# Attention stages of a two-layer streaming encoder: chunks turned and multiplied two at a time, with one PSUM bank for outputs instead of two

## The reference, cut to what matters

```python
def fox_attention_prompt(q, k, v, logf):
    ...
        s = jnp.einsum('bqhd,bkhd->bhqk', qb, k).astype(jnp.float32) * scale
        s = s + cq[..., :, None] - cum[..., None, :]
        ...
        p = jax.nn.softmax(s, axis=-1).astype(v.dtype)
        return jnp.einsum('bhqk,bkhd->bqhd', p, v)

def band_attention_prompt(q, k, v, rel_bias):
    ...
        s = jnp.einsum('bqhd,bkhd->bhqk', qs, ks).astype(jnp.float32) * scale + bias
        ...
        p = jax.nn.softmax(s, axis=-1).astype(vs.dtype)
        return jnp.einsum('bhqk,bkhd->bqhd', p, vs)
```

## Time and profile before

| what | value |
|---|---|
| median of three runs | 3223.16 us (3222.48 to 3224.68) |
| the profiled execution, its own time | 3227.8 us |
| its span, first to last instruction | 3226.0 us |
| PE busy over the span | 3075.5 us, 95% |
| DVE busy over the span | 1371.6 us, 43% |
| ACT, POOL busy | 1062.1 us (33%), 396.3 us (12%) |
| attention phase fox, on PE | 405.9 to 687.5 us |
| attention phase band, on PE | 1997.6 to 2258.6 us |

### The profile page before, as it was taken

One profiled execution on the slowest core, in us unless ns is written; L12 is line 12 of the kernel. 1 busy time (PEld: TensorE's weight loads), 2 busy tenths in 40 slices (PEclk: granted clock), 3 DMA queues, 4 the chain that ended last, 5 costly groups with the idle time before them and its releaser, 6 DMA issues. The chain is left out here.

```text
span 3226.0 us, 49287 instructions
## 1 busy us (share of the span) xinstructions
PE 3075.5 (95%) x16891; PEld 2779.7 (86%) x16891; DVE 1371.6 (43%) x2948; ACT 1062.1 (33%) x2313; POOL 396.3 (12%) x702
## 2 busy tenths in 40 slices
PE   8999699989999999999999998999889999999998
PEld 7877489977899999999978886888779999999998
DVE  3122179962433343333342221888343333333334
ACT  4233178851412121111133232787231111211212
POOL 0000056620000000000000001666010000000001
PEclk9999899999999999999999998999989999999999
DMA  4788165523311111111026875563111111111111
GB/s 152 202 229 237 49 229 211 186 103 100 151 40 44 60 39 52 39 39 39 1 72 187 253 202 174 180 236 134 53 66 53 39 39 39 39 39 39 39 46 59
DMA packets 317139, 337.61 MB, mean 105 GB/s; under 512 B 29009, under 2 KB 260449, under 8 KB 312817
## 3 DMA queue, kind: packets, MB, share of 16 engines
q1 hardware_dynamic: 317040, 336.31, 32.5%
HBM read 238.46 MB, written 111.54 MB: 108 GB/s over the span
## 5 line engine op out<-in xcount | busy, mean ns | idle before, releaser
L230 PE MATMUL ffn_gu<-ffn_xh,ffn_gh 128*128 128x384 f32 x2112 | 708.5, 335 | 0.0
L232 PE MATMUL ffn_gu<-ffn_xh,ffn_gl 128*128 128x384 f32 x2112 | 707.5, 335 | 0.0
L231 PE MATMUL ffn_gu<-ffn_xl,ffn_gh 128*128 128x384 f32 x2112 | 707.1, 335 | 0.0
L1496 ACT ACTIVATE ffn_gate<-ffn_gu 128x384 f32<-128x384 f32 x132 | 65.0, 492 | 1035.4 <-PE ffn_gu L232 1035.3
L230 PEld LDWEIGHTS ffn_gu<-ffn_xh,ffn_gh 128*128 128x128 f32 x2112 | 397.6, 188 | 2.4
L231 PEld LDWEIGHTS ffn_gu<-ffn_xl,ffn_gh 128*128 128x128 f32 x2112 | 397.4, 188 | 2.4
L232 PEld LDWEIGHTS ffn_gu<-ffn_xh,ffn_gl 128*128 128x128 f32 x2112 | 397.2, 188 | 0.0
L1500 DVE TENSOR_TENSOR ffn_gate<-ffn_gu,ffn_gate 128x384 f32<-128x384 f32 x132 | 73.6, 558 | 740.9 <-ACT ffn_gate L1496 740.9
L1523 DVE TENSOR_TENSOR all_h<-ffn_dn,all_h 128x512 f32<-128x512 f32 x396 | 274.0, 692 | 217.3 <-PE ffn_dn L232 217.3
L230 PE MATMUL ffn_dn<-ffn_dh,ffn_hidh 128*128 128x512 f32 x792 | 308.4, 389 | 1.1 <-DVE all_h L1523 1.1
L232 PE MATMUL ffn_dn<-ffn_dh,ffn_hidl 128*128 128x512 f32 x792 | 309.4, 391 | 0.0
(11 more groups left out here) (255 smaller groups left out, 5270.6 us busy)
## 6 DMA issues: line engine op xcount, KB each, us to landing
ffn_graw<-in_w_gate_up SPq DMA_DIRECT2D x40, 1024.0 KB, 7.5
ffn_draw<-in_w_down SPq DMA_DIRECT2D x22, 1024.0 KB, 4.9
fox_ks<-k_split SPq DMA_DIRECT2D x16, 1088.0 KB, 5.6
band_ks<-k_split SPq DMA_DIRECT2D x16, 1088.0 KB, 5.6
qkvw_raw<-in_w_a_in SPq DMA_DIRECT2D x5, 2048.0 KB, 10.2
out<-qkvw_stage SPq DMA_DIRECT2D x36, 256.0 KB, 3.3
q_high<-qkvw_th SPq DMA_DIRECT2D x72, 128.0 KB, 2.4
q_low<-qkvw_tl SPq DMA_DIRECT2D x72, 128.0 KB, 2.4
```

What stands on the lines that cost most here:

```text
L230: pe.matmul(out, xh, wh, start=first, stop=False)
L231: pe.matmul(out, xh, wl, start=False, stop=False)
L232: return pe.matmul(out, xl, wh, start=False, stop=last)
L1496: act.activation(gate[j % GC][:], gu[:, j % GC, 0, 0:SW], ACT.Silu).then_inc(gate_ready, 1)
```

## The change

Within a group every second chunk is now due to be turned at the same tick as the one ahead of it, so that it is multiplied at the same tick too, and the next pair of chunks is due eight ticks later. `tp` gets four banks instead of three, and `op` one instead of two. Nothing else is changed; the number of instructions and their shapes stay.

```diff
     for c, (g, _) in enumerate(chunks):
         ready = max(unit_of[(groups[g][0], i)] for i in groups[g][1]) * TICK + TURN
-        turn_at.append(ready if c == 0 else max(ready, turn_at[-1] + SPACE))
+
+        second = (c - first_chunk[g]) % 2
+        turn_at.append(ready if c == 0 else turn_at[-1] if second else max(ready, free))
+        free = turn_at[-1] + SPACE * (second + 1)
     half_at = [turn_at[c] + HALF for c in last_chunk]
     out_at = [turn_at[c] + WHOLE for c in last_chunk]
...
-    OPS, TPS, PARTS = 2, 3, 5 if fox else 6
+    OPS, TPS, PARTS = 1, 4, 5 if fox else 6
     tp_of = [c % TPS for c in range(C)]
-    if C % TPS == 1:
-        tp_of[C - 1] = 1
+    if C % TPS in (1, 2):
+
+        for x in range(C % TPS):
+            tp_of[C - 1 - x] = TPS - 1 - x
```

## The result

The changed kernel takes 3497.16 us (median of 4 runs, 3489.03 to 3499.81), the kernel before, run beside it, 3222.82 us (3217.31 to 3224.68). The ratio is 1.085, with a 95% interval of 1.0827 to 1.0873: 274 us **slower**. The forecast was 3420 us with a range of 3330 to 3490, so the direction was right and the size was not; the time lies where the clock rival had put it (3490 to 3600).

The account below looks back on a forecast made before the run. PE was taken to set the pace of both phases, DVE close behind. Waits of 85 us (fox) and 74 (band) plus clock falls of 27 and 14 made 200 us on 3227.8; forecast 3420 us, range 3330 to 3490.

Parts of the forecast that it names:

- the clock rival: Rival: the granted clock falls at most waits, near 0.8 in both phases; 3490 to 3600 us, chance 0.12.
- the 159 us of waits: PE's added waits for `whole` with one output bank: 85 us for fox and 74 us for band.
- (6,7) to (0,1): Third handover between groups in a head: PE starts 1.2 us later, within bounds 0 and 1.90.
- (0,1) to (4,5): Fourth handover between groups in a head: PE waits 1.8 us for `whole` behind a maximum and a low part.
- (4,5) to S: Last handover in a head: later scores and a second low part delay `whole`, so S starts 1.67 us late.
- S to (2,3): First handover in a head: PE would start 1.25 us later, when `whole` of S has ended.
- (2,3) to (6,7): Second handover in a head: 0 us taken, within bounds 0 and 2.60, as PE has more work in between.
- The 0.6 us a head: Waits PE already has at the same handovers today, given back: 5.9 us a head becomes net 5.3.
- a merge of two runs: PE's transposes: eight in one run (0.79 us) no cheaper than two runs of four (0.72); taken as nothing.
- one fall a head in band (27 us) and one in two heads in fox (14 us): Clock term: granted clock falls after new PE waits, each fall costing about 1.7 us of work.
- a fall after two waits in each head: Upper bound of the clock term over both phases, 109 us; the lower bound was no fall.
- The rule of the Trainium skill on rotating banks: By it alone each handover exposes the emptying, 0.38 + 0.40 us, 160 times: 125 us, or 3350 us.

Follow-up runs that it names:

- experiment 4: Changed kernel with three transpose banks, plus unneeded matmuls into the free PSUM bank ahead of PE's waits for the output bank: 3425.63 us, ratio 1.0631.
- Experiment 1: Changed kernel's new order alone, with two output banks and three transpose banks as in the kernel before: 3274.4 us, ratio 1.0167.
- experiment 2: Changed kernel's banks alone (one output, four transpose), with the chunk-by-chunk order of before: 3540.64 us, ratio 1.0993.
- experiment 5: Changed kernel with `whole` due one tick earlier on DVE and first in its tick, ahead of the low parts: 3451.17 us, ratio 1.0705.
- experiments 3: Changed kernel with three transpose banks instead of four, one PSUM bank left idle: 3526.73 us, ratio 1.0934.

## Why the prediction was wrong in its size

**Right: what bounds, and the kind of loss.** PE waits for DVE's `att_turned` before first multiplications. Of the 159 us of waits that the sum held for 32 heads, 144 came in the 30 heads of the two stretches. The handovers can be set beside the worked ones in one fox head; PE's timeline there:

```profile
558.50 0.55 PE L1243 MATMUL fox_tp<-all_ident,fox_pr 128*128 128x128 f32 x3 [0.74 <-DVE fox_low L1148]
559.62 0.38 PE L1270 MATMUL fox_op<-fox_high,fox_vs 128*128 128x256 f32 x1 [0.57 <-DVE att_turned L1165]
...
563.32 0.39 PE L1270 MATMUL fox_op<-fox_high,fox_vs 128*128 128x256 f32 x1 [1.99 <-DVE att_turned L1165]
...
564.93 1.72 PE L1243 MATMUL fox_tp<-all_ident,fox_pr 128*128 128x128 f32 x7
566.29 0.78 PE L1214 MATMUL fox_sc_wide<-fox_ks,fox_qh 128*128 128x512 f32 x1
...
571.09 0.53 PE L1261 MATMUL fox_op<-fox_both,fox_vs 128*128 128x256 f32 x1 [1.82 <-DVE att_turned L1165]
```

In this head (6,7) to (0,1) costs 0.74 + 0.57 = 1.31 us, (0,1) to (4,5) 1.99 and (4,5) to S 1.82. Over heads 2 to 16 of each phase the listed waits for `whole` are, in us a head:

| handover | worked | fox | band |
|---|---|---|---|
| S to (2,3) | 1.25 | 0.13 | 0.03 |
| (2,3) to (6,7) | 0 | 0 | 0.42 |
| (6,7) to (0,1) | 1.2 | 0.91, and 0.34 for low parts | 2.28 |
| (0,1) to (4,5) | 1.8 | 1.87 | 0.74 |
| (4,5) to S | 1.67 | 1.63 | 1.99 |

- In fox four of the five terms came as worked.
- In band, which took over the numbers of fox, only (4,5) to S comes near. The sum fits there by luck: 1.1 us more at (6,7) to (0,1) and 1.1 less at (0,1) to (4,5).
- The 0.6 us a head that the sum took as lost already before was too much by the list: before, it has 2.0 us of such waits over the whole fox phase. This makes up for about half a microsecond a head of the wait behind S that did not come.
- POOL's waits ahead of `turn` in band vanished, as taken.

From S to (2,3) 1.25 us were worked and hardly any came, but the order that the term stands for did: PE no longer starts before `whole` of S has ended. In the head shown the last step of S on DVE (L1162) ends at 575.50 and PE starts on (2,3) at 575.73:

```profile
575.22 0.28 DVE L1162 TENSOR_TENSOR att_turned<-fox_whole_out 64x128 f32 x1
...
575.73 0.58 PE L1270 MATMUL fox_op<-fox_high,fox_vs 128*128 128x256 f32 x1
```

PE is at half clock at S (the last window of this head below). Its eight transposes ahead of (2,3) start at 573.89, so they take 1.84 us here, where they took 0.79 before; PE comes as late as DVE, and no wait is listed. The same trace bears this out: the three fox heads in which the list has this wait (0.50, 0.72 and 0.79 us) are those in which these transposes run at full clock. In experiment 4, at a clock of 0.99, PE reaches this place 0.77 us ahead of DVE in most heads. So this term went over into the clock's cost.

What makes the handover from (4,5) to S is on DVE's timeline of the same head: two low parts in a row and the cached sum ahead of `whole`, which PE waits for until 571.09. Ahead of them stands a maximum for which DVE itself had waited 2.13 us, until PE, at half clock, had made the scores; so PE's lateness and its lower clock come back as lateness of DVE.

```profile
568.18 0.82 DVE L1142 CUSTOM_DVE_ANT_0 fox_pr<-fox_sc_wide,fox_ncb 128x640 f32<-128x640 f32 x1 [2.13 <-PE fox_sc_wide L1217]
...
568.93 1.15 DVE L1148 TENSOR_TENSOR fox_low<-fox_tp,fox_high 128x512 fp32r<-128x512 f32 x2
570.00 0.42 DVE L1171 TENSOR_REDUCE fox_cs<-fox_sc_slim 128x128 f32<-128x256 f32 x1
570.45 0.42 DVE L1165 TENSOR_TENSOR att_turned<-fox_op,fox_half_out 64x256 f32 x1
```

**Slightly wrong: "a merge of two runs gives between nothing and a loss of 0.07 us".** That priced PE's side alone. Experiment 1 shows 51 us lost by the order with the banks of before, from DVE's side and from waits between the two runs of a pair. In the sum it hardly counts, since with one output bank the new order is 43 us better than the old one (experiment 2).

**The step that failed: the clock.** The sum held "one fall a head in band (27 us) and one in two heads in fox (14 us)", 41 us. The account shows 114, and that over 15 of the 16 heads of each phase. Windows over the same fox head, in four stretches, of which the third lies in the second:

```profile
555.00:565.00 10.00, 6.70 (x50) 5.96 (x49) 6.79 (x20) 7.19 (x17) 5.67 (x10) 0.97 0.24 88
565.00:571.00 6.00, 4.27 (x25) 3.98 (x24) 3.46 (x11) 1.85 (x5) 2.82 (x4) 0.77 0.00 0
568.00:571.00 3.00, 1.27 (x12) 1.17 (x11) 2.75 (x7) 0.77 (x3) 0.53 (x1) 1.00 0.00 0
571.00:575.00 4.00, 3.91 (x19) 3.92 (x20) 0.74 (x4) 0.38 (x1) 1.20 (x2) 0.52 0.00 0
```

and over a band head:

```profile
2264.00:2267.40 3.40, 3.29 (x14) 3.10 (x14) 0.48 (x2) 1.20 (x5) 1.25 (x2) 0.53 0.00 0
2268.00:2274.00 6.00, 3.85 (x34) 3.67 (x32) 3.77 (x14) 2.66 (x8) 5.02 (x11) 1.00 0.00 0
2274.60:2277.80 3.20, 3.00 (x15) 2.60 (x13) 2.40 (x7) 2.01 (x4) 0.39 (x2) 0.50 0.49 138
```

After waits of 0.74, 0.57 and 1.99 us the granted clock falls: the run of seven transposes from 564.93 takes 1.36 us to the next matmul, where at full clock eight took 0.79. It recovers (1.00 from 568 us on), and after the wait of 1.82 us it is near the lower level (0.52) again through the work on S. That is two falls in this head, and two in the band head. Counted in windows of 0.4 us through both stretches (a fall is a run of windows below 0.75), the clock falls **25 times in 15 fox heads and 29 times in 15 band heads**, where the sum held 8 and 16 for 16 heads each. 36 of these falls cost about 1.7 us each, as that of the earlier trace rows; 18, most of them in fox, last twice as long and cost twice as much. So the number of falls was chosen too low, and for a third of them the price as well. The upper bound that the prediction worked out, a fall after two waits in each head, was 2 x 32 x 1.7 = 109 us; it comes near the measured 114 in part by luck, with more falls at a lower price. The reason given beside the clock rival, that nothing in fox shows a fall yet, was no evidence: the waits listed in fox before were of at most 0.3 us, so no wait of the new size stood there to show one. With the bound itself the sum would have been 3227.8 + 159 + 109 = 3496 us, against 3499.36 measured in the profiled execution. The clock rival had named this, with its time and its sign (a clock near 0.8 in both phases; it was 0.84), at a chance of 0.12.

The rule of the Trainium skill on rotating banks (page "Perfetto Trace Analysis", section "Optimizing Tensor Performance") pointed the right way. The time that was worked out by it, 3350 us, was 147 us too low, for the two things that it says nothing of there: the queue ahead of `whole` (experiment 5) and the clock. On the second the same page of the Trainium skill, section "Matmul Optimizations", says that the matmul engine's power follows its utilization, so that matmuls should run back to back; experiments 3 and 4 agree as far as the granted clock goes, with 0.79 to 0.80 against 0.99.

**Open.** Experiment 4 was made with three banks of `tp`, because the fourth is where its filler writes; what a full clock would be worth in the changed kernel itself is bounded only by the account (114 us) and by that run (101 us net of the filler). The 39 us of clock that the fourth bank is worth are not explained, nor why a fall lasts longer in fox than in band.

## What to carry to other kernels

When a change brings waits of one or two microseconds into every round of an engine that ran almost without any, price both the wait and the lower clock behind it, and take the number of falls from the places where the new waits will stand, not from how often the old trace shows one: a trace without waits is no evidence that the clock holds. The second output bank was worth more (252 us between experiments 1 and 3) than either the longer runs or the fourth bank for transposes; a wait can also hide, where the waiting engine is itself slowed; and the small waits that the kernel before still had were worth more than their listed length.

## What was not expected of the hardware

- Useless matmuls in PE's waits made a kernel 101 us faster (3526.73 to 3425.63 us), because the granted clock rose from 0.80 and 0.79 to 0.99.
- Waits of 0.57 to 1.99 us, four within 13 us, went with a granted clock of 0.77 and then 0.52; over both phases the lower clock cost 114 us beside 144 us of waits.
- Listed waits plus (1 - granted clock) x length gave the growth of five of the six experiments and of the change within 7 us, from -15 to +297 us.
